# Reordering VectorE's queue at the start of the gated MLP

## The chip, the cores and the metric

The kernel runs on one core of a Trainium2 chip. The metric is the device time of one execution in microseconds. TensorE (PE in the views) multiplies matrices into PSUM. VectorE (DVE), ScalarE (ACT) and GpSimd (POOL) do the elementwise work. SyncE (SP) issues the transfers. Each engine works through its own queue in order. Engines wait for each other through semaphores.

## The reference, cut to what matters

Two layers of an encoder run over 1024 + 256 = 1280 tokens of width 1024. The second half of each layer is a gated MLP:

```python
h = rms_norm(x, norm_ffn_pre[l])
u = h @ w_up                                # 1024 -> 2 * 2816
c = conv_b
for i in range(3):                          # centred depthwise convolution over the tokens
    c = c + up[:, i:i + s] * conv_w[i]
gate, val = jnp.split(c, 2, axis=-1)
x = x + rms_norm((gelu(gate) * val) @ w_down, norm_ffn_post[l])
```

## The kernel before

Tokens lie along the free dimension and channels along the partitions. The width of 2816 is cut into 22 pairs of blocks, 128 gate channels and 128 value channels each. Every number is split into a high part (rounded by ScalarE) and a low part (the remainder, by a subtraction), and each product is three matmuls: high by high, low by high, high by low.

The routine `gated_mlp` runs once in each layer. The projection for pair 0 is already in PSUM when it begins. For every pair there are the same steps. ScalarE multiplies by the middle tap and adds the bias ("centre"). VectorE adds the left and the right tap (`taps`, lines 2971 and 2976). ScalarE applies GELU. VectorE multiplies gate by value (`gate`, line 3000). SyncE stores the result from `c_gate`. There is one `c_gate` tile, so ScalarE's centre of pair 1's gate waits until pair 0's product has been stored (`act.wait_ge(act_stored, 16 * j)` in `gate_centre`).

TensorE does pair 1 plainly (`plain`): 72 matmuls for the gate half into banks 6, 7 and 0, and 72 for the value half into banks 3, 4 and 5. Those last banks hold pair 0's value half, so it waits for VectorE's taps on it (`pe.wait_ge(val_shifted, 2)`). From pair 2 on it uses a Strassen-like scheme with seven products in place of eight (`fast_pair`), on the first 1024 tokens. The first product of pair 2 (A11) writes bank 0, from which VectorE's taps on the gate half of pair 1 still read: `pe.wait_ge(gate_shifted, 2 * FAST)`.

The scheme needs four mixed blocks of the activations, made once in a layer. `t_forms(k)` on VectorE (lines 3009 to 3018) makes chunk k of all four, by six subtractions of 128x512; ScalarE rounds them (`t_high`, line 2655), and `t_lows(which, ks)` on VectorE (line 3024) takes the remainders. TensorE waits for the four remainders of block 2 ahead of its second product (`T2_PARTS`).

The queues are written out by hand. ScalarE's begins:

```python
gate_centre(0)
act.activation(c.second_hi[:], c.raw[1][:], ACT.Copy).then_inc(second_hi, 1)
plain_val_centre(0)
for k in range(4):
    t_high(2, k)
    if k == 1:
        gelu(0)
operand(FAST, A11)
operand(FAST, S2)
for k in range(4):
    t_high(3, k)
gate_centre(1)
```

GpSimd's begins with `second_lo` (line 2909), the weight sums S1 and S2 of pair 2 (lines 2882 and 2885), and then, once ScalarE has rounded them, the remainder of A11 (line 2895), the sum S3 (line 2888) and the remainder of S2 (line 2895). The remainder of S3 follows after ScalarE has passed the gate centre of pair 1.

Of the kernel before, what the change touches and what calls it, by code (L numbers as in the profile page):

```python
# [275 lines left out]
def bank(c, b, w=512, rows=slice(0, P), off=0):  # L276
    return c.ps[rows, b * 512 + off:b * 512 + off + w]
# [31 lines left out]
def unit_psum(c, half, t0=0, t1=T, rows=slice(0, P)):  # L309
    return c.ps[rows, half * 1536 + t0:half * 1536 + t1]  # L310
# [1820 lines left out]
def gated_mlp(nc, c, L, final):  # L2131
# [34 lines left out]
    with ExitStack() as ex:  # L2166
# [87 lines left out]
        def act_in(it):  # L2254
            return c.act_first if it == 0 else c.act_in[it % 2]
# [4 lines left out]
        with nc.Block() as block:  # L2260
# [701 lines left out]
            def _(dve):  # L2962
                tapped = [0]

                def taps(j, val, pieces, centred, shifted, units=1):

                    at = j + FF * val
                    dst = c.c_val if val else c.c_gate
                    dve.wait_ge(*centred)
                    for t0, s, src in pieces:  # L2970
                        dve.scalar_tensor_tensor(out=dst[:, t0 + 1:t0 + s], in0=src[:, 0:s - 1], scalar=c.conv[:, 0, at:at + 1],
                                                 in1=dst[:, t0 + 1:t0 + s], op0=ALU.mult, op1=ALU.add).then_inc(left, 1)
                    tapped[0] += len(pieces)
                    dve.wait_ge(left, tapped[0])
                    for t0, s, src in pieces:
                        mm = dve.scalar_tensor_tensor(out=dst[:, t0:t0 + s - 1], in0=src[:, 1:s], scalar=c.conv[:, 2, at:at + 1],
                                                      in1=dst[:, t0:t0 + s - 1], op0=ALU.mult, op1=ALU.add)
                    mm.then_inc(shifted, units)

                def plain_taps(j, val):  # L2980
                    pieces = [(t0, s, unit_psum(c, val, t0, t0 + s)) for t0, s in SEGS]
                    if val:
                        taps(j, 1, pieces, (val_centred, 2 * (j + 1)), val_shifted, 2)
                    else:
                        if j:
                            b = PLAIN_GATE[0]
                            pieces = [(0, 1024, c.ps[:, b * 512:b * 512 + 1024]), (1024, 256, bank(c, PLAIN_GATE[2], 256))]
                        taps(j, 0, pieces, (gate_centred, 2 * j + 2), gate_shifted, 2)
# [8 lines left out]
                def gate(j):  # L2997
                    dve.wait_ge(gelu_done, j + 1)
                    dve.wait_ge(val_shifted, 2 * (j + 1))
                    dve.tensor_tensor(c.c_gate[:], c.c_gate[:], c.c_val[:], ALU.mult).then_inc(gated, 1)  # L3000

                def t_forms(k):

                    b12, b22 = c.my[1][:, k, :], c.my[1][:, 4 + k, :]
                    f1, f2, f3, f4 = (c.t_form[i][:, k, :] for i in (1, 2, 3, 4))
                    h11, l11 = c.hh[:, k, 0:512].bitcast(F32), c.hl[:, k, 0:512].bitcast(F32)
                    h21, l21 = c.hh[:, 4 + k, 0:512].bitcast(F32), c.hl[:, 4 + k, 0:512].bitcast(F32)
                    n = 6 * k
                    dve.tensor_tensor(f1, b12, h11, ALU.subtract).then_inc(t_sums, 1)
                    dve.wait_ge(t_sums, n + 1)  # L3010
                    dve.tensor_tensor(f1, f1, l11, ALU.subtract).then_inc(t_sums, 1)
                    dve.tensor_tensor(f3, b22, b12, ALU.subtract).then_inc(t_sums, 1)
                    dve.wait_ge(t_sums, n + 2)
                    dve.tensor_tensor(f2, b22, f1, ALU.subtract).then_inc(t_sums, 1)
                    dve.wait_ge(t_sums, n + 4)
                    dve.tensor_tensor(f4, f2, h21, ALU.subtract).then_inc(t_sums, 1)
                    dve.wait_ge(t_sums, n + 5)
                    dve.tensor_tensor(f4, f4, l21, ALU.subtract).then_inc(t_sums, 1)

                def t_lows(which, ks):  # L3020
                    for k in ks:
                        done = 4 * (2, 3, 1, 4).index(which) + k + 1
                        dve.wait_ge(t_hi, done)
                        dve.tensor_tensor(c.t_lo[which][:, k, :], c.t_form[which][:, k, :], c.t_hi[which][:, k, :].bitcast(F32),
                                          ALU.subtract).then_inc(t_lo, 1)
# [33 lines left out]
                def low_act(it):  # L3059
                    ah, al = act_tiles(it)  # L3060
                    dve.wait_ge(act_hi, 2 * it + 2)
                    dve.tensor_tensor(al[:, 1, :], act_in(it)[:, 1, :], ah[:, 1, :].bitcast(F32), ALU.subtract).then_inc(act_lo1, 1)

                t_forms(0)
                plain_taps(0, 0)
                t_forms(1)
                plain_taps(0, 1)
                t_forms(2)
                t_forms(3)
                gate(0)  # L3070
                t_lows(2, range(4))
                plain_taps(1, 0)
                t_lows(3, range(4))
                t_lows(1, range(4))
# [280 lines left out]
```

## Time and profile before

| | us |
|---|---|
| median of 3 runs | 3556.62 |
| lowest and highest run | 3554.47, 3556.8 |
| the profiled execution, its own time | 3552.48 |
| its span in the profile | 3550.7 |
| start of `gated_mlp` in the two layers, from the span's start | 921.0, 2673.3 |

The span is what the views below show; 1.78 us of the profiled execution's own time lie around it. Times in the rows are in microseconds from the span's start. The two layers do the same work, so what is read at the first one's start is checked at the second one's.

### The profile page before, as it was taken

To read this page: it belongs to the slowest core of one execution; us is meant where nothing else is said; L and a number is where in the kernel's file an instruction comes from. 1 tells how busy PE (TensorE), PEld (TensorE's weight loads), DVE (VectorE), ACT (ScalarE), POOL (GpSimd) and SP (SyncE) were. 2 spreads that over 40 slices of the span, in tenths; PEclk is the share of its full clock that TensorE was granted. 3 is DMA by queue.
4 is the path that set the end of the run, shared out by engine and by line. 5 is a ranking of instruction groups with operands and counts; after the bars stand their busy time and mean duration, and the time that the engine had idled before them with its cause. 6 is when DMAs were issued, how large, how long until landed. Compare 5 with 4: busy or idle time off the path is not lost. (4 is left out here: it accounts for less than half of the span.)

```text
span 3550.7 us, 47741 instructions
## 1 busy us (share of the span) xinstructions
PE 3451.8 (97%) x17305; PEld 2858.6 (81%) x17305; DVE 2068.9 (58%) x3148; ACT 1715.8 (48%) x2973; POOL 1659.0 (47%) x1239
## 2 busy tenths in 40 slices
PE   8999999999899999999999999999998999999998
PEld 7788777778788888888777887777787888888886
DVE  4234888964745555455651358799366455554555
ACT  4343888974444434411353358789553344343113
POOL 1133554443477676423342435534345776763223
PEclk9999999999999999999999999999999999999999
DMA  5442320122122121422324413211232121213213
GB/s 181 128 104 75 77 75 23 42 84 96 53 68 78 58 78 58 144 80 82 118 70 135 127 52 90 57 34 32 75 107 67 62 78 59 78 58 137 95 66 119
DMA packets 247439, 292.81 MB, mean 82 GB/s; under 512 B 43244, under 2 KB 197182, under 8 KB 247167
## 3 DMA queue, kind: packets, MB, share of 16 engines
q1 hardware_dynamic: 247207, 289.76, 27.0%
q8 instruction: 140, 2.29, 0.3%
q14 instruction: 92, 0.75, 0.1%
HBM read 202.70 MB, written 80.31 MB: 80 GB/s over the span
## 5 line engine op out<-in xcount | busy, mean ns | idle before, releaser
L1709 DVE TENSOR_TENSOR pl<-ps,ph 128x512 fp32r<-128x512 f32 (+1 forms) x576 | 376.4, 654 | 66.4 <-ACT ps L1540 65.9
L1432 PE MATMUL ps<-q,k 97*128 97x512 f32 (+4 forms) x1296 | 387.1, 390 | 17.2 <-DVE pl L1709 7.0
L3098 DVE TENSOR_TENSOR y<-ps,y 128x512 f32<-128x512 f32 (+1 forms) x432 | 260.2, 602 | 230.8 <-PE ps L291 227.7
L1539 ACT ACTIVATE ph<-ps 128x512 fp32r<-128x512 f32 (+1 forms) x576 | 329.2, 572 | 135.2 <-PE ps L1432 130.6
L1540 ACT ACTIVATE ps<-ps 128x512 f32<-128x512 f32 (+1 forms) x576 | 328.4, 570 | 0.0
L1432 PEld LDWEIGHTS ps<-q,k 97*128 97x128 f32 (+2 forms) x1296 | 234.4, 189 | 86.3 <-DVE pl L1709 24.5
L1670 DVE TENSOR_REDUCE mx<-ps 128x1 f32<-128x512 f32 x352 | 242.0, 688 | 40.6 <-PE ps L1461 32.5
L1444 PE MATMUL ps<-ph,vh 128*128 128x512 f32 (+1 forms) x576 | 227.4, 395 | 0.0
L1445 PE MATMUL ps<-ph,vl 128*66 128x512 f32 (+1 forms) x576 | 219.7, 381 | 0.0
L1447 PE MATMUL ps<-pl,vh 128*128 128x512 f32 (+1 forms) x576 | 219.7, 381 | 0.0
L289 PE MATMUL ps<-hh,wh 128*128 128x512 f32 (+1 forms) x528 | 200.5, 380 | 10.1 <-PEq L283 6.2
L1461 PE MATMUL ps<-k,q 128*128 128x512 f32 (+3 forms) x540 | 207.0, 385 | 0.7 <-ACT ps L1540 0.5
L1607 POOL CAST hh<-ot 64x512 fp32r<-64x512 f32 (+1 forms) x96 | 51.3, 535 | 314.2 <-DVE ot L1693 311.6
L2362 PE MATMUL ps<-t_hi,op_hi 128*128 128x512 f32 x480 | 187.4, 390 | 1.1 <-POOL op_lo L2895 1.1
L291 PE MATMUL ps<-hh,wl 128*128 128x512 f32 (+1 forms) x528 | 188.1, 356 | 0.0
L290 PE MATMUL ps<-hl,wh 128*128 128x512 f32 (+1 forms) x528 | 187.8, 356 | 0.0
L2363 PE MATMUL ps<-t_lo,op_hi 128*128 128x512 f32 x480 | 187.2, 390 | 0.0
L2364 PE MATMUL ps<-t_hi,op_lo 128*128 128x512 f32 x480 | 186.8, 389 | 0.0
L2895 POOL TENSOR_TENSOR hl<-raw,hh 128x512 fp32r<-128x512 f32 x80 | 110.9, 1388 | 128.8 <-ACT hh L2650 128.8
L290 PE MATMUL ps<-al_odd,dw_hi 128*128 128x512 f32 (+1 forms) x480 | 170.7, 356 | 0.0
L289 PE MATMUL ps<-ah_odd,dw_hi 128*128 128x512 f32 (+1 forms) x480 | 170.4, 355 | 0.0
L291 PE MATMUL ps<-ah_odd,dw_lo 128*128 128x512 f32 (+1 forms) x480 | 169.8, 354 | 0.0
(396 smaller groups left out, 10193.9 us busy)
## 6 DMA issues: line engine op xcount, KB each, us to landing
activations<-c_gate SPq DMA_DIRECT2D x44, 640.0 KB, 3.8
act_in<-activations SPq DMA_DIRECT2D x20, 1280.0 KB, 5.7
raw<-in_w_up SPq DMA_DIRECT2D x48, 512.0 KB, 4.9
up_raw<-in_w_up SPq DMA_DIRECT2D x40, 512.0 KB, 4.7
raw<-in_w_down SPq DMA_DIRECT2D x40, 512.0 KB, 3.5
heads<-stage SPq DMA_DIRECT2D x28, 640.0 KB, 3.5
rq<-heads SPq DMA_DIRECT2D x56, 320.0 KB, 4.0
raw<-in_w_in SPq DMA_DIRECT2D x32, 512.0 KB, 4.4
```

Of the source, the lines that this page charges most:

```text
L289: pe.matmul(out, wh, xh, start=(k == 0), stop=False)
L290: pe.matmul(out, wh, xl, start=False, stop=False)
L291: last = pe.matmul(out, wl, xh, start=False, stop=(k == len(pairs) - 1))
L1432: mm = pe.matmul(out, a, b, start=(k == 0), stop=(k == len(prods) - 1))
L1444: pe.matmul(out, c.vh[kv(h)][:, kt, :], c.ph[g % RING][:, 0:w], start=first, stop=False)
L1445: pe.matmul(out[0:VL_COLS, :], c.vl[kv(h)][:, kt, :], c.ph[g % RING][:, 0:w], start=False, stop=False)
L1447: pe.matmul(out, c.vh[kv(h)][:, kt, :], c.pl[g % RING][:, 0:w], start=False, stop=last).then_inc(pv_done, 1)
L1539: act.activation(c.ph[g % RING][:, 0:w], scores, ACT.Exp, scale=STEP_SCALE[kind(h)]).then_inc(exp_done, 1)
L1540: act.activation(scores, scores, ACT.Exp, scale=STEP_SCALE[kind(h)]).then_inc(exp_done, 1)
L1670: dve.tensor_reduce(c.mx[:, qt, kb:kb + 1], bank(c, b, w), AX.X, ALU.max).then_inc(max_taken, 1)
L1709: dve.tensor_tensor(c.pl[g % RING][:, 0:w], bank(c, ST + g % 3, w), c.ph[g % RING][:, 0:w].bitcast(F32), ALU.subtract).then_inc(p_low, 1)
L3098: dve.tensor_tensor(y, bank(c, down_bank(it, u), w), y, ALU.add).then_inc(down_added, 1)
```

## The change

Only the order of VectorE's queue at the start of `gated_mlp` changes. No instruction is added or taken away, and no wait is changed.

```diff
+                plain_taps(0, 0)
                 t_forms(0)
-                plain_taps(0, 0)
-                t_forms(1)
                 plain_taps(0, 1)
-                t_forms(2)
-                t_forms(3)
+                for k in range(1, 4):
+                    t_forms(k)
+                t_lows(2, range(4))
                 gate(0)
-                t_lows(2, range(4))
                 plain_taps(1, 0)
                 t_lows(3, range(4))
                 t_lows(1, range(4))
```

The taps on pair 0's gate half now stand ahead of chunk 0 of the mixed blocks, the taps on its value half ahead of chunks 1 to 3, and the four remainders of block 2 ahead of the product of pair 0.

## Rows read from the trace of the kernel before

**Rows 1.** The page: busy time of each engine, share of the span, instructions.
```profile
PE 3451.8 (97%) x17305; PEld 2858.6 (81%) x17305; DVE 2068.9 (58%) x3148; ACT 1715.8 (48%) x2973; POOL 1659.0 (47%) x1239
```

**Rows 2.** TensorE's waits, whole span: total us, times, longest.
```profile
PE ps L289 <- DVE c_val L2976: 6.8, 4, 2.9
PE ps L2362 <- DVE c_gate L2976: 5.8, 2, 2.9
PE ps L2377 <- DVE c_gate L2976: 5.5, 4, 1.5
```

**Rows 3.** Timeline of TensorE, first layer: start, length, work [idle before].
```profile
937.89 0.47 PE L289 MATMUL ps<-hh,second_hi 128*128 128x512 f32 x1 [2.88 <-DVE c_val L2976]
...
956.44 0.76 PE L2362 MATMUL ps<-hh,op_hi 128*128 128x512 f32 x1 [2.89 <-DVE c_gate L2976]
```

**Rows 4.** Timeline of VectorE, first layer.
```profile
923.68 2.77 DVE L3016 TENSOR_TENSOR t_form<-t_form,hh 128x512 f32<-128x512 f32 x1
...
927.09 1.67 DVE L2971 SCALAR_TENSOR_TENSOR c_gate<-ps,params,c_gate 128x1023 f32<-128x1023 f32 x2
...
930.38 0.68 DVE L3009 TENSOR_TENSOR t_form<-my,hh 128x512 f32<-128x512 f32 x1
...
934.37 1.67 DVE L2971 SCALAR_TENSOR_TENSOR c_val<-ps,params,c_val 128x1023 f32<-128x1023 f32 x2
...
945.62 2.59 DVE L3000 TENSOR_TENSOR c_gate<-c_gate,c_val 128x1280 f32<-128x1280 f32 x1
948.14 4.68 DVE L3024 TENSOR_TENSOR t_lo<-t_form,t_hi 128x512 fp32r<-128x512 f32 x4
952.91 1.67 DVE L2971 SCALAR_TENSOR_TENSOR c_gate<-ps,params,c_gate 128x1023 f32<-128x1023 f32 x2
...
956.21 7.30 DVE L3024 TENSOR_TENSOR t_lo<-t_form,t_hi 128x512 fp32r<-128x512 f32 x12
...
995.71 1.49 DVE L3000 TENSOR_TENSOR c_gate<-c_gate,c_val 128x1280 f32<-128x1280 f32 x1
```

**Rows 5.** Timeline of ScalarE, first layer.
```profile
921.00 1.42 ACT L2597 ACTIVATE c_gate<-ps,params 128x1280 f32<-128x1280 f32 x1 [9.79 <-PEq L283]
...
951.22 1.66 ACT L2597 ACTIVATE c_gate<-ps,params 128x1024 f32<-128x1024 f32 x2 [3.17 <-DMA activations<-c_gate]
```

**Rows 6.** Timelines of VectorE and TensorE, second layer.
```profile
2705.21 1.68 DVE L2971 SCALAR_TENSOR_TENSOR c_gate<-ps,params,c_gate 128x1023 f32<-128x1023 f32 x2
...
2708.74 0.47 PE L2362 MATMUL ps<-hh,op_hi 128*128 128x512 f32 x1 [2.92 <-DVE c_gate L2976]
```

**Rows 7.** Timeline of GpSimd, first layer.
```profile
923.44 2.45 POOL L2909 TENSOR_TENSOR second_lo<-raw,second_hi 128x1024 fp32r<-128x1024 f32 x1 [9.11 <-ACT second_hi L2695]
926.69 1.64 POOL L2882 TENSOR_TENSOR first_sum<-up_raw 128x512 f32<-128x512 f32 x1 [0.79 <-DMA up_raw<-in_w_up]
928.41 1.29 POOL L2885 TENSOR_TENSOR first_sum<-first_sum,up_raw 128x512 f32<-128x512 f32 x1
945.52 1.35 POOL L2895 TENSOR_TENSOR op_lo<-up_raw,op_hi 128x512 fp32r<-128x512 f32 x1 [15.81 <-ACT op_hi L2650]
946.95 2.42 POOL L2888 TENSOR_TENSOR up_raw<-up_raw,up_raw 128x512 f32<-128x512 f32 x1
949.33 1.73 POOL L2895 TENSOR_TENSOR op_lo<-first_sum,op_hi 128x512 fp32r<-128x512 f32 x1
961.58 3.09 POOL L2895 TENSOR_TENSOR op_lo<-up_raw,op_hi 128x512 fp32r<-128x512 f32 x1 [10.52 <-ACT op_hi L2650]
```

**Rows 8.** The chain that ended last, second layer, pair 4.
```profile
2763.64 2.21 DVE c_gate L2976 x2
2765.89 0.39 PE ps L2377
```

**Rows 9.** Instructions by the tile t_form: shortest, median and longest in ns.
```profile
L3016 DVE TENSOR_TENSOR t_form<-t_form,hh x8: 691/692/2774, 923.7 to 2696.6; 128x512 f32<-128x512 f32 x8
```

**Rows 10.** The stretch after TensorE's first restart: busy time, TensorE's granted clock.
```profile
938.00:946.00 8.00, 8.00 (x29) 6.37 (x30) 7.79 (x13) 2.35 (x5) 0.48 (x1) 0.79 0.01 3
```

## The prediction

> **What bounds the kernel now.** I read the page first. TensorE is busy for 97% of the span and no other engine for more than 58% [rows 1], so time is lost or won only where TensorE stands still, or where what releases it moves. The waits of TensorE say where: at the start of the MLP it stands twice in each layer for VectorE, once with the value half of pair 1 (the two of 2.9 us among the four waits on c_val) and once with the first product of pair 2 (two, 5.8 us) [rows 2]. The timeline gives the places in the first layer: 2.88 us ahead of 937.89 and 2.89 us ahead of 956.44 [rows 3]. So the first batch of 72 matmuls ended at 935.01, and the second at 953.55.
>
> I then followed back what released each. The first wait ends when VectorE's taps on the value half of pair 0 end. They begin at 934.37 [rows 4], behind two chunks of mixed blocks and the gate taps.
>
> The second wait is what matters. It ends when VectorE's taps on the gate half of pair 1 end. These begin at 952.91 [rows 4], right when ScalarE's centre of that half ends (951.22 + 1.66 = 952.88). That centre had itself stood idle for 3.17 us for the store of pair 0's product [rows 5]. The store could be issued only when the product ended on VectorE, 945.62 + 2.59 = 948.21 [rows 4]. So the second wait hangs on a rigid chain: end of the product, 3.0 us for the store, 1.7 us for the centre, 3.3 us for the taps, TensorE. In numbers: 948.21, 951.22, 952.91, 956.2, 956.44. Call the end of the product G. **TensorE begins the fast pairs at G + 8.2 us.** The second layer has the same distances: taps from 2705.21, TensorE from 2708.74 [rows 6].
>
> Does a shift of that start reach the end? ScalarE's rounding for the remaining operands stands in its queue behind the centre of pair 1, GpSimd's remainders behind that (its operation at 961.58 waited 10.52 us for ScalarE [rows 7]), and VectorE's other remainders behind the taps. All of it is tied to the same moment. In the next two pairs TensorE waits again for VectorE (four waits on c_gate, 5.5 us in all [rows 2]), and the chain that ended last passes through that wait at 2765.89 [rows 8]. After that TensorE sets the pace. No slack stands between the start of the fast pairs and the end, so I count a shift of G once in each layer, in full.
>
> **The change, part by part.** I rebuild VectorE's queue of the first layer, from its start at 921.02 (ScalarE's first centre begins at 921.00 [rows 5]).
>
> The lengths come from starts to next starts [rows 4]. Taps on one half: 927.09 to 930.38, 3.29 us. One chunk of mixed blocks: 930.38 to 934.37, 3.99 us. The product alone: 1.49 us. One remainder alone: twelve take 7.30 us, 0.6 each, 2.4 for four.
>
> *Gate taps first.* They can't start at 921.02; they wait for ScalarE's centre, until 921.00 + 1.42 = 922.42 [rows 5]. VectorE stands idle for 1.43 us there, where it now works. They end at 922.45 + 3.29 = 925.74.
>
> *A stall that goes, and what takes its place.* The 2.77 us of one subtraction at 923.68 are odd: the median of its line is 0.69 [rows 4, 9]. It overlaps GpSimd's second_lo, 923.44 to 925.89 [rows 7], and ends 0.6 us after it. So a VectorE subtraction with both inputs in SBUF stands until GpSimd's operation is over; this costs 2.08 us. Taps, which read PSUM, aren't held: those at 927.09 kept 1.67 us beside GpSimd's sum at 926.69 [rows 4, 7]. After the change second_lo runs beside the gate taps, so the 2.08 us go. But GpSimd's two sums at 926.69 and 928.41 now meet chunk 0 of the mixed blocks (925.74 onward) instead of the taps. Their start is set by a load [rows 7], not by VectorE. Each can hold VectorE for its own 1.29 us. I call this c: between 0 and 2.6. I take 2.6, because the chunk has places where VectorE waits for its own last result, just as at 923.68 where GpSimd got in.
>
> *Value taps.* They start at 925.74 + 3.99 + 2.6 = 932.3 and end at 935.6, against 937.66 now. TensorE's first wait shrinks from 2.88 us to some 0.8, and the slow stretch behind it (granted clock 0.79 over 8 us [rows 10]: part of it at the lower of the two levels) may go. This is a gain of 2 to 4 us for the second batch, which then ends near 949.6 in place of 953.55. It buys nothing if the second wait is then longer.
>
> *Chunks 1 to 3*, 12.0 us: they end at 947.6 (now 945.62).
>
> *Remainders ahead of the product.* Four remainders and the product are 2.4 + 1.49 = 3.9 us alone. In this stretch GpSimd does three operations, in the trace from 945.52, 946.95 and 949.33 [rows 7]. Their start follows ScalarE's rounding of the last chunk, so they come at the same offset after the change. Now they stretch the product from 1.49 to 2.59 us and the four remainders from 2.5 to 4.67 (948.14 to 952.81) [rows 4]: 3.3 us in all, of which 1.1 lie ahead of G. After the change all of it lies ahead of G. I call this w: 3.3, or 1.1 if only the first operation holds VectorE.
>
> The sum for the first layer: G = 921.02 + 1.43 + 2 x 3.29 + 4 x 3.99 + 3.9 + c + w = 948.9 + c + w, against 948.2 now. **The shift is 0.7 + c + w = 0.7 + 2.6 + 3.3 = 6.6 us in each layer, 13.2 in both.** TensorE's second wait becomes some 13.4 us long in place of 2.9.
>
> On the restart's clock I put nothing: in the first layer the fast pairs already began with 0.63 us matmuls in the present trace (0.76 for the first [rows 3]), in the second at full speed (0.47 [rows 6]). Up to 1.5 us for each layer goes into the range.
>
> ScalarE's rounding of block 2, and TensorE's need for its remainders, aren't helped: all four remainders are ready at 952.8 now, and TensorE asks for them only after 956.44. Moving them forward covers nothing.
>
> The profiled execution took 3552.48 us, so it would take 3565.7. That execution is 4.1 us under the median of the runs, 3556.62. On the median the sum is **3569.8 us, 0.37% slower**. I take 0.2% (7.1 us) as what a measurement of this kernel can tell from no change.
>
> **A rule weighed against the rows.** GpSimd's remainder at 961.58 took 3.09 us in place of 1.29 [rows 7], while VectorE ran its twelve remainders without a gap until 963.43. GpSimd stood through about three of them. But at 948.14 to 951.5 VectorE's remainders were held twice. So both happen.
>
> The Trainium skill (SBUF — State Buffer, "SBUF: two separate sides") says that the port pair of the two engines is an exclusive lock: a VectorE operation with two SBUF inputs or a GpSimd operation, whichever starts first, has it for the whole instruction. By that alone each of the five GpSimd operations would be served after at most one VectorE operation, which is my sum of 13.2 us; by the behaviour at 961.58 the sum is less, as in the second rival.
>
> **The rivals.**
>
> *A. VectorE is held at every meeting* (the forecast): c = 2.6, w = 3.3, +13.2 us. A mild form, one of the two sums missing the chunk, c = 1.3, gives +10.6. Together 0.74.
>
> *B. VectorE keeps GpSimd out while it runs without a gap*, as at 961.58. Then w = 1.1: with c = 2.6 the shift is 4.4 us a layer, +8.8, still slower (0.12). With c = 0 it is 1.8 a layer, +3.6 us, 3560.2: **not slower** by what can be measured. It decides from c + w below 2.9 us. For it: the row at 961.58. Against it: the rows at 923.68, 945.62 and 948.14, all of which held VectorE. 0.09.
>
> *C. The second wait isn't tied to G*: if the store or the single c_gate tile didn't release the centre, only the first wait would change, by 2.1 us and up to 1.7 of clock in each layer: -7.6 us, 3549. Against it: ScalarE's 3.17 us wait for exactly that transfer in the first layer. 0.03.
>
> *D. No net effect*, for slack that I haven't seen further on absorbs the shift. Against it: TensorE waits again in the following pairs [rows 2, 8]. 0.02.
>
> **How the numbers follow.** Slower by over 0.2%: A and B's slower form, 0.86. Within 0.2%: B's other form and D, 0.11. Faster: C, 0.03. The time predicted is A's. The range begins at 3562.5, under B's slower form (3565.4) by a part of its way to the other, and ends at 3573.5, the sum plus 1.5 us of clock in each layer and some spread of the runs.
>
> **What would show it.** Right: the taps at L2971 begin near 922.45 in the first layer; no subtraction of a mixed block stands for second_lo, but one or two stand 1.3 us each for the sums L2882 and L2885; TensorE's wait on c_val is under 1 us; the product ends near 954.8; ScalarE's wait for the store grows; the wait of L2362 on c_gate is 12 to 14 us in each layer. Wrong: the product ends before 951, or the fast pairs begin before 959. I would be wrong above all in c and w, and then by 2 to 9 us toward no change.

## The result: 0.34% slower, as forecast

Over nine runs of each the changed kernel took 3567.52 us in the median (3562.43 to 3569.07), the kernel before 3553.61 us (3552.15 to 3556.99). The ratio is 1.0034, with a 95% interval of 1.0024 to 1.0044: by the ratio 12.1 us more, between 8.5 and 15.6; the two medians themselves lie 13.9 us apart. The forecast was 13.2 us more. The profiled execution took 3566.62 us, its span is 3564.7 us.

The two waits of TensorE come first. This is TensorE's timeline of the changed kernel, first layer; the rows answer to [rows 3].

```profile
921.75 0.47 PE L289 MATMUL ps<-hh,mw 128*128 128x512 f32 x1 [1.53 <-PEq L283]
...
936.18 0.47 PE L289 MATMUL ps<-hh,second_hi 128*128 128x512 f32 x1 [0.41 <-DVE c_val L2976]
...
963.26 0.76 PE L2362 MATMUL ps<-hh,op_hi 128*128 128x512 f32 x1 [13.04 <-DVE c_gate L2976]
```

The first wait fell from 2.88 to 0.41 us, the second rose from 2.89 to 13.04. Counted from TensorE's first matmul of the routine (921.75 here, 921.02 before), the fast pairs start at 41.5 us in place of 35.4: 6.1 us later. The second layer shows the same:

```profile
2680.66 0.47 PE L289 MATMUL ps<-hh,mw 128*128 128x512 f32 x1 [1.15 <-PEq L283]
...
2695.09 0.47 PE L289 MATMUL ps<-hh,second_hi 128*128 128x512 f32 x1 [0.43 <-DVE c_val L2976]
...
2722.16 0.77 PE L2362 MATMUL ps<-hh,op_hi 128*128 128x512 f32 x1 [13.06 <-DVE c_gate L2976]
```

VectorE's timeline of the changed kernel tells where the 6.1 us come from; it answers to [rows 4].

```profile
923.19 1.68 DVE L2971 SCALAR_TENSOR_TENSOR c_gate<-ps,params,c_gate 128x1023 f32<-128x1023 f32 x2 [12.44 <-ACT c_gate L2597]
924.90 1.68 DVE L2976 SCALAR_TENSOR_TENSOR c_gate<-ps,params,c_gate 128x1023 f32<-128x1023 f32 x2
926.49 0.68 DVE L3009 TENSOR_TENSOR t_form<-my,hh 128x512 f32<-128x512 f32 x1
927.21 0.69 DVE L3011 TENSOR_TENSOR t_form<-t_form,hl 128x512 f32<-128x512 f32 x1
927.82 1.78 DVE L3012 TENSOR_TENSOR t_form<-my 128x512 f32<-128x512 f32 x1
929.52 1.77 DVE L3014 TENSOR_TENSOR t_form<-my,t_form 128x512 f32<-128x512 f32 x1
...
932.66 1.67 DVE L2971 SCALAR_TENSOR_TENSOR c_val<-ps,params,c_val 128x1023 f32<-128x1023 f32 x2
...
947.89 5.75 DVE L3024 TENSOR_TENSOR t_lo<-t_form,t_hi 128x512 fp32r<-128x512 f32 x4
953.57 1.48 DVE L3000 TENSOR_TENSOR c_gate<-c_gate,c_val 128x1280 f32<-128x1280 f32 x1
959.73 1.67 DVE L2971 SCALAR_TENSOR_TENSOR c_gate<-ps,params,c_gate 128x1023 f32<-128x1023 f32 x2 [4.69 <-ACT c_gate L2597]
```

Four things are to be seen here. VectorE begins when ScalarE's centre ends, 1.44 us into the routine. Two subtractions of chunk 0 take 1.78 and 1.77 us in place of 0.69. The four remainders take 5.75 us, where four take 2.4 when nothing holds VectorE (twelve in a row take 7.30 [rows 4]). The product ends at 955.05, 33.3 us after the start, against 27.2 before; then VectorE, busy without a break in the kernel before, stands idle for 4.69 us.

ScalarE's timeline of the changed kernel, first layer (it answers to [rows 5]):

```profile
958.04 1.66 ACT L2597 ACTIVATE c_gate<-ps,params 128x1024 f32<-128x1024 f32 x2 [7.72 <-DMA activations<-c_gate]
```

and GpSimd's (it answers to [rows 7]):

```profile
924.18 2.40 POOL L2909 TENSOR_TENSOR second_lo<-raw,second_hi 128x1024 fp32r<-128x1024 f32 x1 [10.37 <-ACT second_hi L2695]
927.32 1.73 POOL L2882 TENSOR_TENSOR first_sum<-up_raw 128x512 f32<-128x512 f32 x1 [0.74 <-DMA up_raw<-in_w_up]
929.12 1.62 POOL L2885 TENSOR_TENSOR first_sum<-first_sum,up_raw 128x512 f32<-128x512 f32 x1
947.79 1.34 POOL L2895 TENSOR_TENSOR op_lo<-up_raw,op_hi 128x512 fp32r<-128x512 f32 x1 [17.05 <-ACT op_hi L2650]
```

ScalarE waits for the store 7.72 us, 4.5 longer than before. From the product's end to the centre it is again 3.0 us.

For the comparison of all kernels below I use one mark, read in both layers of the one profiled execution of each kernel. It is the start of the product of A11 with the short segment (line 2377) in pair 5, which TensorE reaches in all of them without a wait, counted from TensorE's first matmul of the routine. In the kernel before it lies at 117.57 and 117.52 us in the two layers, in the changed kernel at 123.65 and 123.66. So 12.2 us of the 14.0 us between the two spans arise in these two stretches. The other 1.8 us lie outside: 0.7 ahead of the first routine, 0.5 between the first layer's mark and the second routine, 0.5 behind the second mark. No order was changed there, and I haven't traced them.

### The profile page after: what moved, and what is told of

The parts are those of the page before. It is cut to its first block and busy times, and to the rows that moved or that the text cites. A ratio compares the mean times of both kernels' runs of the same rounds, so it can differ in the third digit from the quotient of the medians.

```text
span 3564.7 us, 47741 instructions
## 1 busy us (share of the span) xinstructions
PE 3451.4 (97%) x17305; PEld 2858.1 (80%) x17305; DVE 2070.5 (58%) x3148; ACT 1715.9 (48%) x2973; POOL 1657.4 (46%) x1239
## 5 line engine op out<-in xcount | busy, mean ns | idle before, releaser
L1670 DVE TENSOR_REDUCE mx<-ps 128x1 f32<-128x512 f32 x352 | 242.0, 688 | 39.2 <-PE ps L1461 30.9
```

The costliest lines, as they stand in the source:

```text
L1670: dve.tensor_reduce(c.mx[:, qt, kb:kb + 1], bank(c, b, w), AX.X, ALU.max).then_inc(max_taken, 1)
```

## The experiments

All ratios are to the kernel before, from five rounds each. The intervals of `e1_taps_first`, `e3_own_tile`, `e4_pool_waits` and `e7_early_no_pool` contain 1, so their times alone can't be told from no change. There the reading rests on the mark.

### The two halves alone

`e1_taps_first` has only the moved taps:

```diff
-                t_lows(2, range(4))
                 gate(0)
+                t_lows(2, range(4))
```

(against the changed kernel). 

> One half of the change alone: the taps stand as in the changed kernel, the product of pair 0 stays ahead of the remainders of block 2. Theory (the start of the fast pairs hangs on the end G of pair 0's product): the mixed blocks end 26.2 us after the routine's start as in the changed kernel, the product is stretched by one GpSimd operation as before, so G lies at 26.2 + 1.5 + 1.1 = 28.8 us, against 27.2 before: 1.6 us later in each layer, 3.2 us in all, ratio 1.0009. TensorE's wait for the value taps falls from 2.9 to 0.4 us, its second wait grows from 2.9 to some 7 us. Rival C of the prediction (only the first wait counts): 7.6 us faster, ratio 0.9979. Rival (the taps' move carries the loss): near 1.0034.

Measured: 1.0006 (0.9997 to 1.0015). The mark lies at 119.09 us in both layers, 3.1 us later over the two.

`e2_lows_first` has only the moved remainders:

```diff
-                gate(0)
                 t_lows(2, range(4))
+                gate(0)
```

(against the kernel before). 

> The other half alone: the taps stand as before, the four remainders of block 2 go ahead of the product. Theory: the mixed blocks end at 24.6 us as before, then four remainders, the product and all three GpSimd meetings, 7.2 us: G at 31.8 us, 4.6 us later than before in each layer, 9.2 us in all, ratio 1.0026; the first wait stays at 2.9 us, the second becomes some 7.5 us. With the other half this adds up to the 12.2 us of the changed kernel. Rival (remainders were going to be done anyway, in the same busy stretch of VectorE, so their order costs nothing): ratio 1.0000.

Measured: 1.0028 (1.0016 to 1.0039). The mark lies at 122.19 and 122.14 us, 9.2 us later. TensorE's waits in `e1_taps_first`, whole span (us in total, times, longest):

```profile
PE ps L2362 <- DVE c_gate L2976: 17.0, 2, 8.5
PE ps L289 <- DVE c_val L2976: 1.9, 4, 0.6
```

and in `e2_lows_first`:

```profile
PE ps L2362 <- DVE c_gate L2976: 15.4, 2, 9.1
```

3.1 and 9.2 add up to 12.3; the whole is 12.2. The product of pair 0 ends 1.5 and 4.6 us later than before in the first layer, and the mark moves by the same amounts. The moved remainders carry three quarters of the loss, the moved taps a quarter. The taps win 2.5 us a layer at the first wait, and none of it is left after the second.

### Taking the store off the path

`e3_own_tile` gives pair 0's gate half its own tile; what hangs on it:

```diff
+    c.c_first = put("c_first", [P, T], arena)
...
-                    act.wait_ge(act_stored, 16 * j)
+                    if j > 1:
+                        act.wait_ge(act_stored, 16 * j)
...
                 def t_high(which, k):
+                    if which == 1 and k == 0:
+                        act.wait_ge(act_stored, 16)
```

> The changed kernel, but pair 0's gate half has a tile of its own (the space in which the rounded block 1 comes later), so ScalarE's centre of pair 1 no longer waits for the store of pair 0; the wait for the store moves to ScalarE's first rounding of block 1. Theory (the store chain sets the second wait): ScalarE begins the centre at about 28.6 us after the start instead of 36.3, the taps follow the product directly at 33.3 us, and TensorE's second wait falls from 13.0 to some 8.5 us. ScalarE's later queue moves by only 1.5 to 2.5 us, as its rounding of block 1 still waits for the store and the operands S3 and S1 stand behind it, so TensorE should wait again ahead of its third or fourth product; in time 3 to 8 us less than the changed kernel over both layers, ratio 1.0010 to 1.0026 against before. Rival (VectorE's own work, not the store, sets the second wait): wait unchanged at 13 us, ratio 1.0034.

Measured: 1.0004 (0.9995 to 1.0013), mark at 118.91 and 118.90, 2.7 us later than before and 9.5 less than the changed kernel. Its timeline of TensorE:

```profile
958.21 0.77 PE L2363 MATMUL ps<-hh,op_hi 128*128 128x512 f32 x1 [8.30 <-DVE c_gate L2981]
```

of ScalarE:

```profile
949.96 1.64 ACT L2598 ACTIVATE c_gate<-ps,params 128x1024 f32<-128x1024 f32 x2
```

and of VectorE:

```profile
953.30 1.48 DVE L3006 TENSOR_TENSOR c_first<-c_first,c_val 128x1280 f32<-128x1280 f32 x1
954.70 1.66 DVE L2976 SCALAR_TENSOR_TENSOR c_gate<-ps,params,c_gate 128x1023 f32<-128x1023 f32 x2
```

The centre now runs ahead of the product, and the taps follow the product directly. The product itself ends where it did in the changed kernel, 33.3 us after the start. So the store and the single tile are the link that makes the late product dear: 4.7 us a layer, close to four fifths of the loss. I had expected less, since ScalarE's later roundings still wait for the store. They came at 957.77, and TensorE didn't have to wait for them.

### Keeping GpSimd out of the way

`e4_pool_waits` is the changed kernel with two waits for GpSimd:

```diff
+                        if j == FAST:
+                            pool.wait_ge(t_sums, 6)
...
                     pool.wait_ge(op_hi, op(j, q))
+                    if j == FAST and q == A11:
+                        pool.wait_ge(gated, 1)
```

> The changed kernel, but GpSimd keeps out of VectorE's way: its two first sums wait until chunk 0 of the mixed blocks is done (they then run beside the value taps, which read PSUM), and its remainder of A11 with what follows waits until the product of pair 0 is done. Theory (c = 2.2 and w = 3.3 us of the shift are meetings with GpSimd): no operation of VectorE is stretched ahead of G, G at 23.9 + 3.9 = 27.9 us, 0.7 us later than before in each layer, 1.4 in all, ratio 1.0004; TensorE's second wait falls from 13.0 to some 8 us. Rival (the stretched operations only show time that VectorE would lose anyway): ratio 1.0034. Rival (GpSimd's later work then comes too late for TensorE): a new wait of TensorE for op_lo, ratio over 1.001.

Measured: 1.0005 (0.9997 to 1.0014), mark at 118.18 and 118.23, 1.3 us later than before. VectorE's timeline has the lengths back:

```profile
945.64 2.49 DVE L3028 TENSOR_TENSOR t_lo<-t_form,t_hi 128x512 fp32r<-128x512 f32 x4
948.04 1.48 DVE L3004 TENSOR_TENSOR c_gate<-c_gate,c_val 128x1280 f32<-128x1280 f32 x1
```

The fast pairs start at 957.74, 36.1 us after the start of the routine. That is 0.65 us later than before, which is what the term 0.7 of the sum measures; the other 5.5 us a layer are the five meetings with GpSimd.

The term 0.7 isn't the cost of the order by itself. It is the 1.4 us in which VectorE is idle and the 2.4 us of the four remainders, less the 2.1 and 1.1 us of the two meetings that lay ahead of the product in the kernel before. With GpSimd kept out of the way on both sides, the product ends 27.8 us after the start in this kernel and 24.0 in the next one, which has the order of before. So of the 6.1 us a layer, 3.8 are the order, and 2.3 come from the meetings with GpSimd ahead of the product, 5.5 us of them in place of 3.2.

`e5_before_pool` does this to the kernel before (a further wait, for chunk 0, ahead of `second_lo`, and 12 in place of 6 for the sums). 

> The kernel before, VectorE's and ScalarE's queues untouched, only GpSimd kept out of the way: second_lo waits for chunk 0 of the mixed blocks (it then runs beside the gate taps), the two sums for chunk 1 (beside the value taps), the remainder of A11 for the product of pair 0. Theory: the product's end G moves by the two meetings ahead of it, 2.1 and 1.1 us, from 27.2 to 24.0 us after the routine's start, and the fast pairs with it from 35.4 to 32.2 us: 6.4 us faster over both layers, ratio 0.9982. Rival (G is not what counts in the kernel before, VectorE's sum of work is): ratio 1.0000, as the same meetings come after the product. Rival (the delayed second_lo or loads hold TensorE): a new wait, slower.

Measured: 0.9985 (0.9976 to 0.9994), mark at 115.31 and 115.29, 4.5 us earlier. That is faster than before, but less than expected: the fast pairs start 33.2 us after the start of the routine, where 32.2 had been worked out. VectorE's timeline:

```profile
941.35 1.48 DVE L3005 TENSOR_TENSOR c_gate<-c_gate,c_val 128x1280 f32<-128x1280 f32 x1
942.75 5.78 DVE L3029 TENSOR_TENSOR t_lo<-t_form,t_hi 128x512 fp32r<-128x512 f32 x4
948.46 1.66 DVE L2976 SCALAR_TENSOR_TENSOR c_gate<-ps,params,c_gate 128x1023 f32<-128x1023 f32 x2
```

The product ends 24.0 us after the routine's start (918.83), just as worked out. The centre would have let the taps go at G + 4.7 = 947.5. But the three operations that GpSimd had put off now meet the four remainders, and these end only when the taps start, at 948.46. The chain behind G had 0.1 us of room for the remainders; I had overlooked that it was so little.

### The product early

`e6_early_product` turns the idea around. VectorE's queue:

```python
plain_taps(0, 0); t_forms(0); plain_taps(0, 1); t_forms(1)
gate(0)
t_forms(2); t_forms(3)
plain_taps(1, 0)
t_lows(2, range(4)); t_lows(3, range(4)); t_lows(1, range(4))
plain_taps(1, 1)
t_lows(4, range(4))
gate(1)
```

ScalarE's `gate_centre(1)` moves behind `t_high(2, 2)`, and its rounding of S3 and S1 ahead of `t_high(1, 0)`; GpSimd's sums wait for `t_sums` 6, its remainder of A11 for `t_sums` 24. 

> The opposite of the change for the product: both taps first as in the changed kernel, but the product of pair 0 directly behind chunk 1, the gate taps of pair 1 ahead of all remainders, the remainders of block 4 last; ScalarE centres pair 1's gate after the third rounding of block 2 and rounds S3 and S1 before block 1; GpSimd's sums wait for chunk 0, its remainder of A11 for chunk 3. Theory: G at 17.5 us after the start, store over at 20.5, centre at 22.4, chunk 3 done at 25.5, taps at 28.8, TensorE begins the fast pairs at 29.0 us against 35.4 before, with a second wait under 1.5 us: 6.4 us a layer, 12.8 in all, ratio 0.9964, if TensorE then finds its later operands ready (value taps at 39 us, S3 at 31 us); if GpSimd or VectorE is late there, half of it, ratio 0.998. Rival (the fast pairs' start isn't what sets the end): ratio 1.0000.

Measured: 0.9977 (0.9968 to 0.9986), faster than both kernels. The fast pairs start at 951.15, 28.9 us after the start (922.27), as worked out: 6.5 us earlier a layer. At the mark (113.85 and 113.82) 3.7 us of them are left. TensorE's timeline shows where the rest went:

```profile
951.15 0.47 PE L2362 MATMUL ps<-hh,op_hi 128*128 128x512 f32 x1 [1.07 <-DVE c_gate L2981]
956.49 0.47 PE L2362 MATMUL ps<-t_hi,op_hi 128*128 128x512 f32 x1 [0.91 <-DVE t_lo L3029]
964.60 0.47 PE L2362 MATMUL ps<-t_hi,op_hi 128*128 128x512 f32 x1 [2.38 <-DVE c_val L2981]
974.96 0.47 PE L2362 MATMUL ps<-hh 128*128 128x512 f32 x1 [1.62 <-DVE u_val L3049]
```

Three waits stand behind the first, 4.9 us in all, each for VectorE; in the same stretch of its first layer the kernel before has two, 1.15 and 1.52 us. VectorE's timeline tells why it is late:

```profile
950.92 10.25 DVE L3029 TENSOR_TENSOR t_lo<-t_form,t_hi 128x512 fp32r<-128x512 f32 x12
961.09 1.66 DVE L2976 SCALAR_TENSOR_TENSOR c_val<-ps,params,c_val 128x1023 f32<-128x1023 f32 x2
...
964.37 5.75 DVE L3029 TENSOR_TENSOR t_lo<-t_form,t_hi 128x512 fp32r<-128x512 f32 x4
970.05 2.58 DVE L3005 TENSOR_TENSOR c_gate<-c_gate,c_val 128x1280 f32<-128x1280 f32 x1
```

The twelve remainders take 10.25 us instead of 7.30, the last four 5.75 instead of 2.4, the product of pair 1 2.58 instead of 1.49: 7.4 us more in all, beside GpSimd's work of the same stretch. So the meetings kept off the start come back behind it. An estimate from these rows: without the 2.95 us in the twelve remainders, the taps on the value half would end some 39.2 us after the start. TensorE comes to its wait for them at 40.0 us, so the wait of 2.38 us would all but go. No run leaves these meetings out, so this isn't shown.

`e7_early_no_pool` is the same order without GpSimd's waits. 

> As the early product, without the waits given to GpSimd: the order of the queues alone. Theory: chunk 0 is held for 2.2 us by the two sums and a later subtraction for up to 1.1 us by the remainder of A11, so the fast pairs start at 31.2 to 32.3 us: 6 to 8.4 us faster than before in all, ratio 0.9976 to 0.9983. Rival (GpSimd's early start is worth as much to TensorE as VectorE loses by it): the same time as with the waits.

Measured: 0.9997 (0.9988 to 1.0006): no gain that can be told from no change, where I had expected 6 to 8 us. The start of the fast pairs was as expected, 952.83 or 31.1 us after the routine's start (921.76). But behind it TensorE waited for VectorE again, among others:

```profile
965.93 0.47 PE L2362 MATMUL ps<-t_hi,op_hi 128*128 128x512 f32 x1 [1.62 <-DVE c_val L2977]
976.30 0.47 PE L2362 MATMUL ps<-hh 128*128 128x512 f32 x1 [3.25 <-DVE u_val L3045]
```

The mark lies at 117.23 and 118.34. An early start is worth only what VectorE's later work allows.

`e8_corner_first` takes the last of those waits away from the early product, by splitting the last four remainders:

```diff
-                t_lows(4, range(4))
+                t_lows(4, range(2))
+                second_sum(FAST)
+                third_sum(FAST)
+                corner22(FAST)
+                t_lows(4, range(2, 4))
                 gate(1)
```

The loop over the pairs then leaves these three sums out for pair 2. 

> The early product with its new late wait mended: TensorE stood 1.6 us in each layer for corner 22 of pair 2, which VectorE reached only behind the remainders of block 4 and the product of pair 1; here VectorE does the three sums of pair 2 between the second and the third of those remainders. Theory: that wait goes, nothing else moves, 1.6 us a layer or 3.2 in all less than the early product, ratio near 0.9968 against before. Rival (VectorE's sum of work is what binds from there on, so the wait reappears ahead of the product A22 or in pair 3): ratio 0.9977, as the early product had.

Measured: 0.998 (0.9971 to 0.9989), the same as the early product within the intervals. The mark lies at 114.16 and 113.28. TensorE's timeline no longer has the wait for u_val; two others stand further on:

```profile
984.37 0.39 PE L2377 MATMUL ps<-hh,op_hi 128*128 128x256 f32 x1 [0.46 <-DVE c_gate L2981]
...
1011.01 0.39 PE L2377 MATMUL ps<-hh,op_hi 128*128 128x256 f32 x1 [1.52 <-DVE c_gate L2981]
```

The theory that the wait would simply go fell; the rival, that it comes back further on, is what the rows show.

## Why the prediction was right, point by point

- *The second wait hangs on the end of pair 0's product.* Right, and shown three ways. The halves move the product's end and the mark by the same amounts; a tile of its own takes the loss down from 12.2 to 2.7 us, with the product no earlier; a product at 24.0 us in the kernel before wins time.
- *The gate taps wait for ScalarE.* Forecast 1.43 us, measured 1.44.
- *The 2.08 us stall goes.* Right: no subtraction stands for `second_lo`, which ran beside the gate taps in 2.40 us.
- *c = 2.6.* Measured 2.2: chunk 0 took 6.17 us (926.49 to 932.66) against 3.99. Two sums each held one subtraction, but for 1.09 us, not for the sum's own 1.29; what makes the difference isn't settled. My reason for taking the upper end of c was wrong, so the choice was right by luck: I said GpSimd gets in where VectorE waits for its own last result. It got in at L3012 and L3014, which began with no such gap behind the instruction before.
- *w = 3.3.* From 947.89 to 955.05 it is 7.16 us, less 3.9: 3.3.
- *The sum.* 0.7 + 2.2 + 3.3 = 6.2 a layer, measured 6.1. The surplus of the forecast is c, but for 0.1 us. The term 0.7 is itself a difference, 3.84 us of order less 3.18 of meetings; the sum had both parts right, and only the experiments tell them apart.
- *No slack behind.* Right for the mark: the 6.1 us at the start of the fast pairs are 6.1 at pair 5. On the way TensorE's clock cost something that was given back. Busy time by engine from the restart on, with the granted clock in the last column but two, of the changed kernel:

```profile
963.00:969.00 6.00, 5.74 (x16) 4.61 (x17) 6.00 (x11) 5.85 (x9) 0.60 (x1) 0.52 0.00 0
```

and of the kernel before:

```profile
956.00:962.00 6.00, 5.56 (x23) 4.70 (x24) 6.00 (x11) 5.67 (x9) 0.42 (x1) 0.72 0.00 0
```

After the wait of 13 us TensorE did 16 matmuls in six microseconds at a granted clock of 0.52, almost all of it at the lower of the two levels, against 23 at 0.72, a mixture of both. In the first layer it released VectorE's sum into u_val 1.0 us later, counted from the restart (978.45 - 963.26 = 15.2 us, against 970.62 - 956.44 = 14.2). VectorE's timeline of the changed kernel, and then of the kernel before:

```profile
978.45 0.69 DVE L3044 TENSOR_TENSOR u_val<-ps,part_b 128x512 f32<-128x512 f32 x1 [1.71 <-PE ps L2364]
```

```profile
970.62 0.69 DVE L3044 TENSOR_TENSOR u_val<-ps,part_b 128x512 f32<-128x512 f32 x1 [0.71 <-PE ps L2364]
```

In pair 3 the kernel before waits for the gate taps, as TensorE's timeline shows:

```profile
986.97 0.39 PE L2377 MATMUL ps<-hh,op_hi 128*128 128x256 f32 x1 [1.15 <-DVE c_gate L2976]
```

The changed kernel doesn't wait there at all in the first layer, and for 0.63 us against 1.28 in the second. Counted from the start of the fast pairs, TensorE begins this short segment after 30.5 to 30.6 us in both layers of both kernels, and of `e1_taps_first` to `e5_before_pool` too. So the wait took the loss in. Putting nothing on the clock was right for the sum, but the prediction didn't see this wait as the reason: that was luck.

- *The rivals.* B (GpSimd kept out) did not come about ahead of the product. C is refuted by the experiments with the halves and by the measured sign, D by the mark.

In `e6_early_product` the lower of the two gains that the expectation gives came about, and in `e8_corner_first` the rival. Three expectations missed altogether. In `e5_before_pool` and `e7_early_no_pool` I followed the chain to the start of the fast pairs and not far enough to VectorE's work behind it; in `e3_own_tile` I looked there for a wait that didn't come.

## What to carry to other kernels

Where one tile is worked on, stored and used again, the last operation on it ahead of the store can be part of the critical path of what comes next. Other work then belongs behind it in its engine's queue, not ahead of it, as far as the work put off isn't needed soon itself (`e7_early_no_pool` won nothing). A shorter first wait is no gain while a second wait behind it hangs on another chain; follow what ends the last wait of the stretch, and look at a mark further on before counting it. When an operation is moved, look at which operations of the other engines it will now run beside: of the 6.1 us a layer that was 2.3, and without it the loss would have been 3.8.

## What the runs showed of the hardware

A VectorE operation with both inputs in SBUF and a GpSimd operation shut each other out, while VectorE's taps, which read one input from PSUM, ran beside GpSimd in their usual 1.67 to 1.68 us. Each meeting cost VectorE 1.09 us with a 128x512 operation on both sides. The rows for the taps are those at 924.90 beside GpSimd's operation at 924.18. Which of the two has to stand doesn't seem to be only a matter of who came first, as far as the profile's times of GpSimd can be trusted, which are rough. In the changed kernel, too, GpSimd's remainder of S3 stood through about three of twelve remainders on VectorE that ran without a gap (3.09 us in place of 1.29). VectorE's timeline:

```profile
963.03 7.30 DVE L3024 TENSOR_TENSOR t_lo<-t_form,t_hi 128x512 fp32r<-128x512 f32 x12
```

and GpSimd's:

```profile
968.40 3.09 POOL L2895 TENSOR_TENSOR op_lo<-up_raw,op_hi 128x512 fp32r<-128x512 f32 x1 [15.90 <-ACT op_hi L2650]
```

The Trainium skill (SBUF — State Buffer, "SBUF: two separate sides") gives the pair of ports to whichever starts first, for the whole instruction. The meetings in chunk 0 agree with it; by this row's times a waiting GpSimd operation needn't be the next one served, of which the page says nothing. What decides between the two stays open.
